# Retention samples' query: from state-as-weights with one moving column to q-as-weights with the state moving, two samples in two column groups

## The reference, cut to what matters

```
decay = 1, xi = gamma_h, zeta = 1, g_c = gamma_h
a     = einsum('bnhk,bmhk->bhnm', q, k) * decay
o     = einsum('bhnm,bmhv->bnhv', a, v) + einsum('bnhk,bhkv->bnhv', q, s) * xi
s_new = g_c * s + einsum('bmhk,bmhv->bhkv', k * zeta, v)
```

## Time and profile before

| | |
|---|---|
| median of 3 runs | 1893.29 us (1892.6 to 1895.07) |
| profiled execution, its own time | 1892.95 us |
| its span in the trace | 1891.2 us |
| mean granted clock of TensorE | 0.982 |
| TensorE busy, matmuls / weight loads | 95% / 92% |
| VectorE, ScalarE, GpSimd busy | 55%, 48%, 41% |
| query matmuls L1631 | 512 records, 64.2 us busy |
| t_last L1048 and t_first L542 | 64 each, about 0.75 and 0.67 us each |

### The profile page before, as it was taken

The page is one execution under the profiler, slowest core; times in us unless marked ns, Lnnn a source line. Parts: engine busy times, 40 slices in busy tenths (PEclk is TensorE's granted clock), DMA queues, the critical chain, the costliest instruction groups (busy, mean ns, idle before and its releaser), DMA issues.

```text
span 1891.2 us, 32237 instructions
## 1 busy us (share of the span) xinstructions
PE 1805.9 (95%) x13996; PEld 1731.5 (92%) x13996; DVE 1041.9 (55%) x1124; ACT 911.6 (48%) x1064; POOL 774.0 (41%) x225
## 2 busy tenths in 40 slices
PE   8999989999979999899999978999999999999997
PEld 7999989999969999888989868999999998999997
DVE  4454555675386753545555555676244545467743
ACT  4555555444454444444444445443455565544443
POOL 4554535555314444322122101455364454444441
PEclk9999989999989999999999989999999999899999
DMA  8767854555424556745545522455668667545552
GB/s 271 248 221 267 282 197 145 180 177 175 148 90 158 179 184 197 224 158 165 164 140 164 156 78 90 156 178 164 212 205 288 222 231 271 180 134 179 180 182 85
DMA packets 306035, 346.31 MB, mean 183 GB/s; under 512 B 7847, under 2 KB 269479, under 8 KB 305887
## 3 DMA queue, kind: packets, MB, share of 16 engines
q1 hardware_dynamic: 257968, 260.36, 43.4%
q10 hardware_dynamic: 47927, 83.90, 12.7%
HBM read 299.66 MB, written 44.82 MB: 182 GB/s over the span
## 4 chain that ended last, share of the span: by engine, by line
PE 82%; DVE 9%; ACT 4%; issue 3%; DMA 1%; ACTq 1%; PEldq 0%; DVEq 0%
PE acc L1491 21%; PE acc L1492 20%; PE acc L1498 20%; PE mix L1631 2%; PE mix L1889 2%; PE mix L1553 1%; PE acc L1519 1%; ACT w_hi L433 1%; PE acc L1520 1%; DVE w_lo L925 1%; PE acc L1525 1%; PE mix L1643 1%; PE mix L1862 1%; PE mix L1720 1%; DMA st<-in_state_ret_dram 1%
## 5 line engine op out<-in xcount | busy, mean ns | idle before, releaser
L1398 POOL TENSOR_TENSOR w_lo<-raw,w_hi 128x2048 fp32r<-128x2048 f32 (+2 forms) x162 | 690.2, 4265 | 688.9 <-ACT w_hi L433 688.9
L1491 PE MATMUL acc<-g_hi,w_hi 128*128 128x264 f32 x2544 | 639.8, 289 | 8.6 <-DVE gate L1182 2.9
L1492 PE MATMUL acc<-g_lo,w_hi 128*128 128x264 f32 x2544 | 628.9, 284 | 0.0
L433 ACT ACTIVATE w_hi<-raw 128x2048 fp32r<-128x2048 f32 (+3 forms) x260 | 455.8, 1755 | 162.3 <-PE acc L1498 79.2
L925 DVE TENSOR_TENSOR w_lo<-raw,w_hi 128x2048 fp32r<-128x2048 f32 (+2 forms) x98 | 381.0, 3888 | 266.7 <-ACT w_hi L433 266.7
L1491 PEld LDWEIGHTS acc<-g_hi,w_hi 128*128 128x128 f32 x2544 | 479.4, 188 | 18.5 <-issue 13.7
L1492 PEld LDWEIGHTS acc<-g_lo,w_hi 128*128 128x128 f32 x2544 | 482.0, 189 | 1.3
L1498 PE MATMUL acc<-g_hi,w_lo 128*128 128x264 f32 x2544 | 343.7, 285 | 0.6 <-POOL w_lo L1398 0.6
L1498 PEld LDWEIGHTS acc<-g_hi,w_lo 128*128 128x128 f32 x2544 | 325.9, 188 | 3.6 <-issue 1.3
L1431 POOL TENSOR_TENSOR h_lo<-hid,h_hi 128x528 fp32r<-128x528 f32 x44 | 59.2, 1345 | 332.7 <-ACT h_hi L707 332.7
L704 ACT ACTIVATE silu_gate<-gate 128x528 f32<-128x528 f32 x44 | 28.4, 646 | 283.6 <-DVE gate L1182 283.6
(11 more groups left out here) (241 smaller groups left out, 2400.1 us busy)
## 6 DMA issues: line engine op xcount, KB each, us to landing
raw<-in_w_ffn_in_dram SPq DMA_DIRECT2D x88, 1024.0 KB, 5.3
raw<-in_w_in_ret_dram SPq DMA_DIRECT2D x48, 1024.0 KB, 6.9
raw<-in_w_in_attn_dram SPq DMA_DIRECT2D x36, 1024.0 KB, 5.7
st<-in_state_ret_dram ACTq DMA_DIRECT2D x64, 512.0 KB, 6.7
out_dram<-st ACTq DMA_DIRECT2D x64, 512.0 KB, 6.1
raw<-in_w_ffn_out_dram SPq DMA_DIRECT2D x32, 768.0 KB, 4.3
raw<-in_w_ffn_out_dram SPq DMA_DIRECT2D x32, 640.0 KB, 4.6
raw<-in_w_out_ret_dram SPq DMA_DIRECT2D x16, 1024.0 KB, 6.7
```

The lines of the kernel that those rows point to most:

```text
L433: A(w_hi[:, u % SPL, 0:size[u]], raw[:, u % RAW, 0:size[u]], ACT.Copy).then_inc(hi_split, 1)
L1398: TT(w_lo[:, u % SPL, 0:size[u]], raw[:, u % RAW, 0:size[u]], w_hi[:, u % SPL, 0:size[u]].bitcast(F32), ALU.subtract).then_inc(lo_by_pool, 1)
L1491: MM(out, wh, x_hi[:, ks[k], :], start=first and k == 0, stop=False)
L1492: MM(out, wh, x_lo[:, ks[k], :], start=False, stop=False)
```

## The change

The query no longer goes through tq. q of a head's eight samples is copied by VectorE, once per head, into q_two, a small zeroed tile (zeroed by GpSimd once per layer) in which each sample has a pair of columns, one of them zero. The new query(n) is issued for n even and serves samples n and n+1: for each of the two halves kt of the state's rows, two matmuls with two columns of q_two as the stationary operand and the 512 state columns moving, sample n in column group n % 4 and sample n+1 in the next one. Two samples of a head, n and n+4, share a group: the second has its q in the other column, and the sums add up in rows 32 j and 32 j + 1 of mix bank 3. After the fourth pair ScalarE copies the bank to o_rows (sample_rows, with the factor 1/16), TensorE turns it with four transposes into mix bank 0 (turn_samples), and sample_out picks the eight columns per block. t_first and t_last are gone, with them t_ready; qs_done is raised once per pair, and load_to waits for it, for the pair of the slot's sample. The query waits for st_updated of both its samples.

In the order of the code, units 1 to 3 of a head now hold query, spread, spread at places 0, 1 and 2; unit 0 is as it was. Unit 4 holds the last query at place 0 and the turn at place 1, and gn_mean stands behind the unit. In the tail similar moves are made by hand.

```diff
-                            act.wait_ge(t_ready, g - ST + 1)
+                            act.wait_ge(qs_done, (g - ST) // 2 + 1)
...
-                def t_first(n):
-                    g = 32 * r + n
-                    act.wait_ge(st_updated, g + 1)
-                    if g:
-                        act.wait_ge(t_ready, g)
-                    b = n % 8
-                    if b == 0:
-                        act.wait_ge(s1_ready, RH * r + n // 8 + 1)
-                    A(mix[:, 3, :], st[:, g % ST, 0, :], ACT.Copy, scale=rq[:, n // 8 % 2, 0, SEQ + b:SEQ + b + 1])\
-                        .then_inc(t_first_ready, 1)
...
+                def sample_rows(gh):
+                    act.wait_ge(qs_done, 4 * (gh + 1))
+                    A(o_rows[:], mix[:, 3, :], ACT.Copy, scale=1.0 / 16).then_inc(o_rows_ready, 1)
+
                 def sample_out(gh, par):
-                    act.wait_ge(qs_done, 8 * (gh + 1))
-                    A(oT[:, par, :, SEQ:T], mix[:, 0, 0:32].rearrange("p (v b) -> p v b", v=4), ACT.Copy,
-                      scale=1.0 / 16).then_inc(os_ready, 1)
+                    act.wait_ge(os_turned, gh + 1)
+                    turned = mix[:, 0, :].rearrange("p (v j x) -> p v j x", v=4, j=4)[:, :, :, 0:2]
+                    A(oT[:, par, :, SEQ:T].rearrange("p v (i j) -> p v j i", i=2), turned, ACT.Copy)\
+                        .then_inc(os_ready, 1)
...
                               scale=zeta[:, h:h + 1]).then_inc(kz_ready, 1)
 
                     if h:
+                        sample_rows(gh - 1)
+                    hi(ub + 6)
+                    if h:
                         sample_out(gh - 1, 1 - par)
-                    hi(ub + 6)
                     if h:
                         load_to(8 * h + 4)
                         gn_square(h - 1)
...
-                def t_last(n):
-                    g, b = 32 * r + n, n % 8
-                    dve.wait_ge(t_first_ready, g + 1)
-                    if g:
-                        dve.wait_ge(qs_done, g)
-                    STT(tq[:], st[:, g % ST, 1, :], rq[:, n // 8 % 2, 1, SEQ + b:SEQ + b + 1], mix[:, 3, :],
-                        ALU.mult, ALU.add).then_inc(t_ready, 1)
...
-                            if s:
-                                t_last(n - 1)
                             update(n)
-                            t_last(n)
                             update(n + 1)
                         evac(s)
+                        if s == 0:
+                            if h == 0:
+                                dve.wait_ge(q_two_zeroed, r + 1)
+                            dve.wait_ge(acc_read, pb + 1)
+                            if gh >= 2:
+                                dve.wait_ge(qs_done, 4 * (gh - 1))
+                            nc.vector.tensor_copy(
+                                q_two[:, par].rearrange("p k (i x) -> p k i x", i=2)[:, :, :, 0:8:2],
+                                rq[:, par, :, SEQ:T].rearrange("p k (i j) -> p k i j", i=2)).then_inc(q_two_ready, 1)
...
                 nc.gpsimd.memset(v_stack[:].bitcast(F32), 0.0).then_inc(stack_zeroed, 1)
+                nc.gpsimd.memset(q_two[:], 0.0).then_inc(q_two_zeroed, 1)
...
                 def query(n):
-                    g, gh, b = 32 * r + n, RH * r + n // 8, n % 8
-                    if b == 0:
-                        pe.wait_ge(o_ready, 2 * gh + 2)
-                    pe.wait_ge(t_ready, g + 1)
+                    gh, par = RH * r + n // 8, n // 8 % 2
+                    half = n % 8 // 4
+                    if n % 8 == 0:
+                        pe.wait_ge(q_two_ready, gh + 1)
+                    pe.wait_ge(st_updated, 32 * r + n + 2)
+                    for kt in range(2):
+                        for i in range(2):
+                            j = n % 4 + i
+                            at = 8 * half + 2 * j
+                            ins = MM(mix[32 * j:32 * j + 2, 3, :], q_two[:, par, kt, at:at + 2],
+                                     st[:, (32 * r + n + i) % ST, kt, :], start=(half == 0 and kt == 0),
+                                     stop=(half == 1 and kt == 1), tile_position=(0, 32 * j))
+                    ins.then_inc(qs_done, 1)
+
+                def turn_samples(gh):
+                    pe.wait_ge(o_rows_ready, gh + 1)
+                    pe.wait_ge(o_ready, 2 * gh + 2)
                     for vt in range(4):
-                        ins = MM(mix[:, 0, vt * 8 + b:vt * 8 + b + 1], tq[:, vt * P:(vt + 1) * P], ones[:, 0:1],
-                                 start=True, stop=True)
-                    ins.then_inc(qs_done, 1)
-
-                def sample(n):
-                    if n % 8 >= 2:
-                        query(n - 2)
-                    spread(n)
+                        ins = TR(mix[:, 0, vt * P:(vt + 1) * P], o_rows[:, vt * P:(vt + 1) * P], ident)
...
-                        if h and s < 4:
-                            samples = (lambda: sample(n), None, lambda: sample(n + 1))
+                        if h and s == 0:
+                            samples = (lambda: spread(n), None, lambda: spread(n + 1))
+                        elif h and s < 4:
+                            samples = (lambda: query(n - 2), lambda: spread(n), lambda: spread(n + 1))
                         elif h and s == 4:
-                            samples = (lambda: query(8 * h - 1), None, lambda: gn_mean(h - 1))
+                            samples = (lambda: query(n - 2), lambda: turn_samples(gh - 1))
                         elif h:
...
                             ins.then_inc(tk_done, 1)
-                            if h:
-                                query(n)
                         if s == 4:
                             pe.wait_ge(acc_read, pb + 4)
                             pe.wait_ge(kz_ready, gh + 1)
                             if h:
-                                pe.wait_ge(st_updated, 32 * r + 8 * h)
-                                pe.wait_ge(t_ready, 32 * r + 8 * h)
+                                gn_mean(h - 1)
                             for j, bank in enumerate((1, 3)):
                                 for t in range(2):
...
-                def second(n, part):
-                    sample(n)
-                    part(3)
+                def both(first, second):
+                    first()
+                    second()
 
                 proj(uo, po, ro_hi, ro_lo, first_half, last=False,
-                     between=(lambda: sample(24), lambda: second(25, gn_mean), lambda: sample(26)))
-                sample(27)
+                     between=(lambda: spread(24), lambda: both(lambda: spread(25), lambda: gn_mean(3)),
+                              lambda: spread(26)))
+                query(24)
+                spread(27)
                 proj(uo + 1, po + 1, ro_hi, ro_lo, first_half, last=False,
-                     between=(lambda: sample(28), lambda: second(29, gn_variance), lambda: sample(30)))
-                sample(31)
+                     between=(lambda: spread(28), lambda: both(lambda: query(26), lambda: spread(29)),
+                              lambda: both(lambda: spread(30), lambda: gn_variance(3))))
+                query(28)
+                spread(31)
                 pe.wait_ge(ro_lo_ready, 5 * r + 3)
                 proj(uo + 2, po, ro_hi, ro_lo, pieces[0], first=False, last=False, done=False,
-                     between=(lambda: query(30), None, lambda: query(31)))
+                     between=(None, lambda: query(30)))
                 proj(uo + 3, po + 1, ro_hi, ro_lo, pieces[0], first=False, last=False, done=False,
-                     between=(lambda: gn_mean(3, True), None, lambda: gn_variance(3, True)))
+                     between=(lambda: turn_samples(RH * r + 3), lambda: gn_mean(3, True)))
+                gn_variance(3, True)
```

25 lines of the change are left out of this document (8 added, 17 removed).

## The result

| | before | after |
|---|---|---|
| median | 1893.05 us (1892.6 to 1895.07) | 1938.24 us (1933.19 to 1943.21) |
| profiled execution | 1892.95 us | 1933.19 us |
| its span | 1891.2 us | 1931.4 us |
| predicted | | 1911.5 us (1897 to 1925) |

The ratio of the times is 1.0232, with an interval of 1.0216 to 1.0249. The direction was right, and the size was not: +45 us where +18 had been worked out. (The median of before counts one execution more than the one given ahead of the prediction.)

The account below looks back on a forecast made before the run. TensorE, busy 95% of the span, was taken to bound the kernel. Pairs +6.3, turn +3.2, spreads +14.2, tq waits -3.9 and tails -1.4 summed to +18.4 us: forecast 1911.5 us, range 1897 to 1925.

Parts of the forecast that it names:

- The step that failed: Unit 4: ScalarE's o_rows copy and the second copy of the turned columns lie beside TensorE's matmuls, costed at nothing.
- The pair: New two-sample query on TensorE: two column groups run side by side, 2.04 us a pair; +6.3 us over six heads.
- The spreads: Units 1 to 3: second spread waits for VectorE's state update, 0.79 us each, 18 times, +14.2 us.
- The turn: Four transposes per head on TensorE, 0.43 us plus 0.1 for the change back to f32r; +3.2 us.
- The tq waits: TensorE's waits for the first tq in heads 2 and 3 go away, 0.98 us four times, -3.9 us.
- The heads together: Length of whole heads in the retention layers: heads 2 and 3 longer by about 3.0 us each, head 1 about 3.9.
- The tails: Last samples beside the out projection: added TensorE work hides in waits; -1.4 us for two, bounds -16 and +6.
- That the clock falls behind new waits: Rival: TensorE slows after each of 18 spread waits, a microsecond each, giving 1930 us; chance 0.05.
- That state slots come late: Rival: stores take 2 us longer, ScalarE's chain slides, units 2 to 4 wait; +13, 1924 us; chance 0.11.
- A cheap pair: Rival: a query pair costs 0.9 us, like one old query, giving 1884 us; decides below about 1.1; chance 0.04.

Follow-up runs that it names:

- Experiment 1: The changed kernel with sample_out put back ahead of the hi split on ScalarE in unit 4: 1909.73 us, 1.0088 of before.
- Experiments 8 and 9: Changed kernel, sample_out ahead of hi, unit 3's last scale_to moved; 8: query right behind first spread, 1897.03 us; 9: spread, query, spread, 1897.44 us.
- experiment 3: The kernel before with only the hi split moved ahead of sample_out on ScalarE in unit 4: 1932.24 us, 1.0204 of before.
- experiment 4: The changed kernel with units 1 to 3 reordered to spread, query, spread: 1941.06 us, 1.0253 of before.
- experiment 7: Changed kernel with four column groups, sample_out ahead of hi, query right behind the first spread, unit 3's last scale_to left until behind the turn: 1879.95 us.

## Why the prediction was wrong, step by step

**The step that failed** is the one on the turn: ScalarE's o_rows copy and "the second copy of the turned columns lie beside the sixteen w_hi matmuls [...] I cost them at nothing". I asked whether these copies would be late for TensorE's turn. They weren't: the turn at 171.43 has no wait, and the w_lo matmuls behind it (sixteen, where the prediction says eight) follow without a gap. I didn't follow what else stands in ScalarE's queue. The change puts hi between o_rows and sample_out, and hi is what releases GpSimd; the diff shows it in plain sight. From there two steps are missing: GpSimd's split starts just ahead of gn_first, and gn_first is an instruction that this split blocks. The prediction's sum has no term for it, and none of its five rivals is it. What the runs showed in its place is a wait of 3.27 us ahead of gn_mean in each of six heads, 19.6 us, and the clock behind some of them.

Could the profile before have shown it? Yes, though in a row that the prediction doesn't use. The line for q_xi, a VectorE product with two SBUF inputs, on 256 columns (minimum/median/maximum in ns), and one instance of it beside GpSimd:

```profile
L1101 DVE TENSOR_TENSOR q_xi<-rq,tret x8: 413/1743/4726, 38.0 to 1567.2; 128x256 f32<-128x256 f32 x8
...
145.05 4.60 POOL L1398 TENSOR_TENSOR w_lo<-raw,w_hi 128x2048 fp32r<-128x2048 f32 x1 [4.43 <-ACT w_hi L433]
...
148.19 1.74 DVE L1101 TENSOR_TENSOR q_xi<-rq,tret 128x256 f32<-128x256 f32 x1
```

An instruction of fixed size whose longest run is eleven times its shortest is not computing all that time. GpSimd ends at 149.65, q_xi at 149.93, 0.28 us later. There it delays nothing: no engine waits for q_xi. With this row the forecast could have been: gn_first ends at GpSimd's start plus 4.55 plus some 0.5 us, TensorE's sixteen w_lo matmuls take 1.95, so about 3 us of wait in six heads, 18 to 20 us, and 1930 in place of 1911.

**The rest of the sum held.** Experiment 1 is the changed kernel without the collision, and its 1909.73 us are 2 us from the forecast. Term by term, from its heads or those of the changed kernel:

- *The pair*: predicted 2.04 us. Measured 82.04 to 83.86, 1.82 us, and with the transitions ahead and behind 0.21 and 0.23 us, which is 2.02 us by the same count as for L1927. The groups run side by side, as in rows 5.

```profile
81.83 0.28 PE L1477 MATMUL acc<-g_lo,w_hi 128*128 128x264 f32 x1
82.04 1.88 PE L1620 MATMUL mix<-st,q_two 128*2 128x512 f32 x8
83.86 0.39 PE L1476 MATMUL acc<-g_hi,w_hi 128*128 128x264 f32 x1
84.09 0.28 PE L1477 MATMUL acc<-g_lo,w_hi 128*128 128x264 f32 x1
```

- *The spreads*: predicted 1.89 us from one to the next, and 0.69 us of wait plus 0.10 around it. The rows show 76.81 to 78.71, 1.90 us, with 0.54 us of wait; the summary of waits has 24 of them, 15.0 us with those of the tails. Experiments 8 and 9 put the whole term at 14 us, with the reserve given there.

```profile
76.81 0.40 PE L1607 MATMUL mix<-v_stack,sel 128*128 128x512 f32 x1
77.04 1.13 PE L1483 MATMUL acc<-g_hi,w_lo 128*128 128x264 f32 x8
78.71 0.50 PE L1607 MATMUL mix<-v_stack,sel 128*128 128x512 f32 x1 [0.54 <-DVE st L1034]
```

- *The turn*: 171.43 to 171.78 is 0.35 us, for 0.43 predicted with 0.1 around it. *The tq waits* at the start of heads 2 and 3 are gone.
- *The heads together*: experiment 1 has 61.05 to 61.09 us in all six, so +3.7 in head 1 (predicted +3.9) and +2.7 in heads 2 and 3 (predicted +3.0).
- *The tails*: -0.9 and -3.2 us in experiment 1, for -0.7 each. The second was under-estimated, within the bounds given.

**The rivals.** That the clock falls behind new waits was given 0.05. It does fall, though not behind the half-microsecond waits that the rival spoke of: it falls behind three of the six waits of 3.27 us and behind all six of 4.9 us. As an amplifier of the true cause it made three heads of the changed kernel 1.5 us longer each, and cost some 13 us in experiment 3. That state slots come late didn't happen in the changed kernel: its stores landed in 4.8 us by the page (6.1 before), and ScalarE waited 15.6 us for landings in all (9.5 before, 55.0 in experiment 4). It happened as soon as the query moved half a unit down (experiment 4), where it made o_rows late and used up what the spreads gave. A cheap pair is real with four groups, some 1.2 us by the prediction's count, and so near its point of decision of about 1.1 but not under it; two groups took 2.02. That the rival's 1884 us lie so close to the 1879.95 us of experiment 7 is luck: the rival has a pair of 0.9 us and keeps the 14 us between the spreads, and experiment 7 has a dearer pair and no such waits.

**What stays open.** Why the clock falls behind a wait in one head and not in another that looks alike, and whether it also makes the difference between the executions of the changed kernel. Experiment 7's heads and tails are shorter by 18 us together and its profiled execution by 15.2; of the difference 2.7 us lie behind the second tail, where nothing was changed, and weren't followed up. For the four-group kernel it wasn't tried which of the two moves was needed; with two groups it was the scale_to.

## What to carry to other kernels

When an edit swaps two instructions on one engine, follow each of them to the engine that it releases, and then ask whether the two released engines now run at the same time; price that pair, not only the wait for it. Look through the profile for instructions of one shape whose longest duration is many times the shortest: another engine may be holding them up, as here, and a kernel may avoid that by its order alone, as the one before did for gn_first. And before hiding a wait by moving its producer, look at what that producer frees (here a state slot), since a gain on TensorE that ends in front of a landing is no gain.

## What the runs showed of the hardware

- A VectorE TENSOR_TENSOR with both inputs in SBUF (128x528), started 0.1 to 0.4 us behind a GpSimd split of 128x2048, took 4.69 to 5.00 us instead of 0.71, in all twelve heads of the changed kernel and experiment 3; started ahead of it, GpSimd not yet running, it took 0.71. A VectorE instruction with one input in PSUM ran through the same split in its usual 1.26 us.
- Eight fp32 records of 512 moving columns took 1.82 us in two column groups and 0.99 us in four, from the first record to the next matmul; with rows 4, 0.43 us a record on the full array, that would be 3.44 us one after the other. The slower steps ahead and behind add 0.20 us in both. Thirty-two stationary columns in place of two cost nothing that shows.
- After waits of equal length (3.27 us) TensorE came back at the full 2.4 GHz in three heads and not in three others: a granted clock of 1.00 and of 0.79 over 8 us, and in the latter 0.50, 1.2 GHz, for some 3 us of them. After 4.86 us, in experiment 3, it stood at 0.50 for the 4 us around the end of the wait, and it fell to 0.50 behind such a wait in all six heads.
